# The decayed keys' product of the HGRN2 scans on GpSimd in place of VectorE

## The reference, cut to what matters

```
b = jnp.cumsum(lc, axis=2)
rel = jnp.where(mask, b[t] - b[s], -inf)
A = einsum('bhtk,bhtsk,bhsk->bhts', qc, exp(rel), kc)
o = einsum('bhts,bhsv->bhtv', A, ic) + einsum('bhtk,bhkv->bhtv', qc * exp(b), S)
S = exp(b_last) * S + einsum('bhsk,bhsv->bhkv', kc * exp(b_last - b), ic)
```

## Time and profile before

| | |
|---|---|
| median of 3 runs | 6358.01 us (6354.26 to 6366.23) |
| profiled execution, span | 6353.6 us |
| its mean granted TensorE clock | 0.953 |
| latent scans, from the first to the last instruction | about 105 to 115 us each, four of them |
| context scans | about 30 to 45 us each, four of them |

### The profile page before, as it was taken

One profiled execution on the slowest core, in us unless ns is written; L12 is line 12 of the kernel. 1 busy time (PEld: TensorE's weight loads), 2 busy tenths in 40 slices (PEclk: granted clock), 3 DMA queues, 4 the chain that ended last, 5 costly groups with the idle time before them and its releaser, 6 DMA issues. The chain is left out here.

```text
span 6353.6 us, 92326 instructions
## 1 busy us (share of the span) xinstructions
PE 5330.7 (84%) x34024; PEld 3653.6 (58%) x34024; DVE 4249.6 (67%) x8349; ACT 2378.9 (37%) x5563; POOL 1901.1 (30%) x1837
## 2 busy tenths in 40 slices
PE   7979889997868888888789798899988788888886
PEld 6759777776753333333277687777766533333332
DVE  3147676886687777767731476768876877777777
ACT  1123672223414444444412136622243244444444
POOL 0002434432223333333300034244312333333332
PEclk8989999999989999999999899999989899999999
DMA  8833117866559999999976431278626699999998
GB/s 342 322 150 135 63 63 256 302 244 215 193 212 420 421 421 421 420 417 417 416 278 230 156 131 60 79 254 296 239 100 215 250 421 421 421 421 419 418 416 344
DMA packets 296533, 1813.71 MB, mean 285 GB/s; under 512 B 35120, under 2 KB 58864, under 8 KB 141940
## 3 DMA queue, kind: packets, MB, share of 16 engines
q0 software_dynamic: 221184, 1342.28, 53.1%
q1 hardware_dynamic: 74902, 465.54, 19.2%
HBM read 1792.74 MB, written 17.04 MB: 285 GB/s over the span
## 5 line engine op out<-in xcount | busy, mean ns | idle before, releaser
L2115 PE MATMUL ex_ps_y<-early,peer_small 128*128 128x512 f32 x1632 | 793.4, 615 | 201.5 <-ACT peer_small L2065 199.0
L2115 PE MATMUL ex_ps_y<-ring,peer_small 128*128 128x512 f32 x1632 | 788.8, 611 | 197.0 <-ACT peer_small L2065 195.0
L1956 DVE CUSTOM_DVE_ANT_0 early<-early,ex_ps_h 128x1024 f32<-128x1024 f32 x408 | 498.0, 1220 | 301.8 <-DMA early<-in_peer_uv,ex_index 298.0
L1956 DVE CUSTOM_DVE_ANT_0 ring<-ring,ex_ps_h 128x1024 f32<-128x1024 f32 x408 | 497.8, 1220 | 282.6 <-DMA ring<-in_peer_uv,ex_index 279.2
L2057 ACT ACTIVATE ex_act<-ex_dot 128x1 f32<-128x1 f32 x1024 | 205.5, 201 | 1261.4 <-DVE ex_dot L1956 1260.2
L2115 PEld LDWEIGHTS ex_ps_y<-early,peer_small 128*128 128x128 f32 x1632 | 288.4, 193 | 625.1 <-issue 624.7
L2115 PEld LDWEIGHTS ex_ps_y<-ring,peer_small 128*128 128x128 f32 x1632 | 285.6, 191 | 616.8 <-issue 616.5
L1692 POOL DMA_INDIRECT early<-in_peer_uv,ex_index x408 | 394.0, 966 | 642.0 <-PE ex_ps_y L2115 567.7
L1692 POOL DMA_INDIRECT ring<-in_peer_uv,ex_index x408 | 389.3, 954 | 645.4 <-PE ex_ps_y L2115 583.5
L2353 POOL DMA_INDIRECT ctx_rows<-in_peer_uv,ctx_iu x256 | 308.6, 1205 | 822.6 <-DMA rec_bounds<-lb_rows 256.2
L2361 POOL DMA_INDIRECT ctx_rows<-in_peer_uv,ctx_iv x256 | 317.9, 1242 | 744.5 <-DVE ctx_y L2390 359.6
(11 more groups left out here) (575 smaller groups left out, 12955.0 us busy)
## 6 DMA issues: line engine op xcount, KB each, us to landing
ring<-in_w_in SPq DMA_DIRECT2D x75, 2048.0 KB, 9.3
ci_w<-in_w_in SPq DMA_DIRECT2D x35, 2048.0 KB, 10.3
ring<-in_w_branch SPq DMA_DIRECT2D x23, 2048.0 KB, 9.1
ring<-in_mod_w SPq DMA_DIRECT2D x22, 2048.0 KB, 8.3
room<-in_peer_wq SPq DMA_DIRECT2D x14, 1024.0 KB, 25.6
co_w<-in_w_out SPq DMA_DIRECT2D x4, 2048.0 KB, 14.9
ring<-in_peer_wq SPq DMA_DIRECT2D x4, 2048.0 KB, 13.7
co_w<-in_peer_wq SPq DMA_DIRECT2D x4, 2048.0 KB, 8.2
```

What stands on the lines that cost most here:

```text
L1956: V.tensor_tensor_reduce(out=row, in0=row, in1=ps_h[:], scale=1.0, scalar=0.0, op0=ALU.mult, op1=ALU.add, accum_out=dot[n % 2][:, s:s + 1] ...
L2115: last = nc.tensor.matmul(ps_y[n % 2][:, c:c + 512], diag[s % DIAGS], v_row[slot(n, s)][:, c:c + 512], start=s == 0, stop=s == TOPK - 1)
```

## The change

`decayed` leaves VectorE's program for GpSimd's. `decayed(0)` is issued after the first clamps and ahead of `carrying(0)`; `decayed(g + 1)` directly behind `carrying(q)` at even q, ahead of `clamp(g + 3)`. Its waits and its semaphore are the same as before.

```
             @block.gpsimd
+                def decayed(g):
+                    pool.wait_ge(turned, g + 1)
+                    if g:
+                        pool.wait_ge(rest_ready, g)
+                    nc.gpsimd.tensor_tensor(k_dec[g % 3][:], k_dec[g % 3][:], group(kk, g), ALU.mult).then_inc(kdec_done, 1)
...
                 clamp(1)
                 if GROUPS > 2:
                     clamp(2)
+                decayed(0)
                 for q in range(PAIRS):
                     carrying(q)
+                    if q % GP == 0 and q // GP + 1 < GROUPS:
+                        decayed(q // GP + 1)
                     if q % GP == 0 and q // GP + 3 < GROUPS:
                         clamp(q // GP + 3)
...
             @block.vector
-                def decayed(g):
-                    dve.wait_ge(turned, g + 1)
-                    if g:
-                        dve.wait_ge(rest_ready, g)
-                    V.tensor_tensor(k_dec[g % 3][:], k_dec[g % 3][:], group(kk, g), ALU.mult).then_inc(kdec_done, 1)
...
                 low(1)
-                decayed(0)
                 times(0)
                 for q in range(PAIRS):
                     g = q // GP
                     if q + 1 < PAIRS:
                         times(q + 1)
-                    if q % GP == 0 and g + 1 < GROUPS:
-                        decayed(g + 1)
                     if q % GP == 0 and g + 2 < GROUPS:
                         low(g + 2)
                     assemble(q)
```

More of the change, by code:

```diff
@@ L1477, in low @@
                     low_part(nc, lf_low[g % 2][:], lf[:], lf_high[g % 2][:]).then_inc(low_done, 1)
[L1479 to L1483, removed]
                 def side_of(q):
```

## The result

The changed kernel takes 6362.97 us (median of 20 runs, 6356.79 to 6372.12), the kernel before 6352.34 us (20 runs, 6339.53 to 6368.13). The ratio is 1.0017, 95% interval 1.0010 to 1.0023: about 10.6 us slower, between 6 and 15. Forecast was +5.2. So it is slower than before, clear of the noise in both, and inside the 0.2% that the prediction called no change. The span of the profiled execution is 6361.8 us, 8.2 more than before.

The account below looks back on a forecast made before the run. VectorE was taken to bound the latent scans, with ACT and TensorE only 5% behind. Latent scans +7.6 and context scans -2.4 gave +5.2 us on 6358.0, so 6363, range 6346 to 6376.

Parts of the forecast that it names:

- The base: Time of the kernel before, median of three runs, 6358.0 us, to which the forecast change was added.
- 24 steady pairs: Latent scans, q = 2, 4, ... 12: GpSimd's moved product starts 0.04 us before VectorE's copy, 0.11 before its big product.
- q = 2: Latent scans, one of the steady pairs: VectorE loses more than it sheds, +0.46 us.
- the first one has it all: When GpSimd's and VectorE's products meet, they don't overlap: whichever issues first keeps the port and the other waits.
- The pair's balance: Steady latent pair: VectorE sheds 0.60 us and loses 1.03 to 1.09, so +0.43 to +0.49, taken as +0.46.
- The special pair q = 10: One per latent scan: a present loss of 0.4 us at the mask product goes, leaving net about +0.1.
- The context scans: At q = 0 the second product runs while VectorE is idle: 0.60 us gained a scan, -2.4 for four.
- q = 0 of the latent scans: Start of each latent scan: GpSimd's first product held by VectorE's big product, a gain of about 0.5 us.
- q = 12: Latent scans, last of the steady pairs: +0.46 us like the others.
- Rival 1: VectorE goes first in the steady pairs and GpSimd is held: net -0.3 us a pair, 6346; chance 0.14.
- Rival 2: The moved product costs VectorE nothing; TensorE and ACT limit the gain to about 0.45 a pair, 6342; chance 0.05.
- Rival 3: TensorE's longer waits in the scans bring more clock falls, 3.5 us each; four more give 6377; chance 0.19.

Follow-up runs that it names:

- f1_change: The changed kernel unaltered, run again on one more chip, against the kernel before: 6364.41 us, ratio 1.0018.
- e8_early_first_on_vector: GpSimd's product issued half a group earlier, each scan's first product left on VectorE, against the kernel before: 6350.73 us, ratio 0.9988.
- e6_three_late: The changed kernel with three small fills ahead of GpSimd's product from group 2 on, against the kernel before: 6362.28 us, ratio 1.0012.
- e2_left_out: The kernel before with VectorE's decayed product cut to one column of 512, the rest left out: 6343.98 us, ratio 0.9978.
- e7_fills: The kernel before plus two unused GpSimd fills of 128x448 in the moved product's place: 6354.05 us, ratio 1.0002.
- e5_one_late: The changed kernel with one small fill ahead of GpSimd's product from group 2 on, against the kernel before: 6367.48 us, ratio 1.0019.
- e3_second_product: The kernel before, VectorE keeping its product, plus an unused 128x448 GpSimd product in the moved product's place: 6373.68 us, ratio 1.0025.

## Why the prediction was right

The time was right by more than its working deserved. 6363 was forecast and 6363.0 measured, but the forecast stood on a base of 6358.0 and +5.2, and the runs have 6352.3 and +10.6. The base was 5.7 too high and the sum 5.4 too low; that the two cancel is luck.

*Right, step by step.* GpSimd's duration (1.27 forecast, 1.28). That it comes first in all 24 steady pairs: before the copy by 0.11 to 0.12 us at q = 2 and by 0.04 to 0.05 in the others (0.04 forecast). That the first one has it all. The pair's balance: the prediction took +0.46 out of +0.43 to +0.49, and the groups have +0.50. That this isn't accident: VectorE's copy of the outputs and GpSimd's carried product wait for the same outputs, and the distance is the same in all steady groups from q = 4 on. The special pair q = 10: +0.1 forecast; from the big product of pair 10 to that of pair 12 the first and the third scan took 11.29 and 11.35 us before, 11.39 both after, and the mask product there is back at 0.42. The context scans: the second product is held by the pending big product (3.06 us at 328.77) and the interval shrinks from 5.14 to 4.54, by the 0.60 forecast.

*Mis-sized, first term: q = 0 of the latent scans,* forecast -0.5. From GpSimd's first instruction in the stage to the third big product the four scans took 19.73, 18.19, 19.55 and 18.47 us before, and 19.80, 18.26, 19.82 and 18.88 after. That is +0.1 in the first two; the last two spread as much between runs of one kernel (the changed kernel again, f1_change, has 19.64 and 19.84). So the term is about +0.1. (Counted from VectorE's first instruction, as in the expectation of e8_early_first_on_vector, the second scan before has 17.7, only because VectorE began 0.45 us late there.) Two things were missed. I had GpSimd's first product held by the big product, from the place of the carried product in the earlier trace rows. But VectorE's own `decayed(0)` no longer delays GpSimd's `clamp`, so the product comes earlier, ahead of the copy, and holds it (first lines below). And ACT works without a pause there, so that what VectorE sheds turns into a wait for ACT, 0.51 us (the last). Timeline of the first latent scan after, to set beside the earlier trace rows:

```profile
651.88 1.28 POOL L1405 TENSOR_TENSOR scan_kdec<-scan_kdec,room 128x512 f32<-128x512 f32 x1
651.95 1.23 DVE L1496 COPY scan_decay<-scan_x 128x2 f32<-128x2 f32 x1 [2.31 <-ACT scan_x L1459]
...
653.10 2.01 DVE L1497 TENSOR_TENSOR scan_x<-scan_x,ring 128x1792 f32<-128x1792 f32 x1
653.12 2.58 POOL L1412 TENSOR_TENSOR scan_carried<-scan_x,main 128x256 f32<-128x256 f32 x1
...
662.27 0.52 DVE L1496 COPY scan_decay<-scan_x 128x2 f32<-128x2 f32 x1 [0.51 <-ACT scan_x L1459]
```

e8_early_first_on_vector separates the two: with `decayed(0)` back on VectorE the first copy is at 0.36 again, and the third big product comes no sooner. So ACT's work is what counts.

*Mis-sized, smaller: q = 2,* forecast +0.46. From the big product of pair 2 to that of pair 4 the second and third scan took 11.88 and 11.83 us before, 12.23 and 12.17 after: +0.3 (0.35 and 0.34).

*Mis-sized, second term: q = 12,* forecast +0.46. From the big product of pair 12 to that of pair 14 it took 10.4 us before and 11.3 to 11.5 after in the first and third scan, which have no fall of the clock there, +0.9 to +1.1. The carried product of the odd pair now meets the mask product, which I had seen for q = 10 of the kernel before and not asked for here. VectorE and GpSimd after:

```profile
3902.93 0.98 DVE L1505 TENSOR_TENSOR scan_part<-scan_summed,scan_bmask 128x256 f32<-128x256 f32 x1
```
```profile
3902.91 0.72 POOL L1412 TENSOR_TENSOR scan_carried<-scan_x,main 128x256 f32<-128x256 f32 x1 [3.02 <-PE scan_ps_o L1374]
```

With the measured sizes the sum is, for a latent scan, 0.1 (q = 0) + 0.3 (q = 2) + 3 x 0.5 + 0.1 (q = 10) + 1.0 (q = 12) = 3.0, and 4 x 3.0 - 4 x 0.6 = +9.6, against 10.6 measured. The agreement is better than the interval of 6 to 15 can prove. The two profiled executions can't test the sum as a whole: their eight scans take 588.4 us before and 594.4 after, only 6.0 more, while the time at the lower clock within them fell from 132 to 118 us. The sum is of stretches that the clock left alone, or in which it was low about as long in both kernels (q = 0, q = 2 and the context scans).

*The rivals.* Rival 1 (VectorE first) had the wrong price: it was -0.3 a pair, and e6_three_late shows +0.5, since the turn goes to GpSimd at the end of the big product. Rival 2 (no cost to VectorE) took 0.45 us a pair as what TensorE and ACT let through; e2_left_out has 0.16 in the middle of a scan. Rival 3: the two profiles show no further falls of the clock. The stretches at the lower level (1.2 GHz of 2.4) sum to less after than before, within the eight scans (118 us against 132) and over the kernel (570 against 596).

*A slip in the working.* With 1.12 us for the product the prediction put its sum at "about 2 instead of 6"; its own sum of 5.2 less 3.6 is 1.6.

*The port.* The runs have the copy, the big product, `low` and the mask product each held by a GpSimd product, and no two-input product held by e7_fills, which only writes. By the rule of the Trainium skill, page "SBUF — State Buffer", section "Who interferes with whom", the two-input products had to behave so, and the runs agree. A quarter of the 4497 ns of the Trainium skill, page "GPSIMD Engine Reference", section "Performance versus the Vector engine", gave an estimate of 1.12 us for the product; the trace has 1.28.

## What to carry to other kernels

Moving elementwise work from a full VectorE to an idle GpSimd isn't judged by busy shares but by what VectorE runs in the same microsecond. Put a GpSimd product with SBUF inputs where VectorE either is in a long product of two SBUF inputs that is followed by instructions with at most one, or idle; half a group's shift turned +12 us into -9. And when an engine is the limit with the next two 5% behind, ask of each microsecond taken from it how much they let through: here 0.16 of 0.53 us in the middle of a scan.

## What the runs showed of the hardware

- The turn is passed on at the end of an instruction to the engine that is already waiting: GpSimd after VectorE's big product (`low` 1.78 in place of 0.68, e6_three_late), VectorE's pending copy after a GpSimd operation (0.36). Being first gains nothing if the next instruction needs the turn too.
- A copy of 128x2 from SBUF to SBUF is held by a GpSimd product for its whole length (1.27 us), and for 0.27 more than its 0.16 even by fills (e7_fills); the two-input product behind it isn't held by fills.
- A shift of 0.06 us decides which of the two waits: GpSimd's product 0.07 us ahead of the big product goes first (e5_one_late), 0.01 ahead it is held (e6_three_late).
- A GpSimd product of 128x448 whose two inputs are the same took 0.94 us (e3_second_product), where the line through products of two tensors says 1.13.
